# Low-rank gate products alternate over two column groups of TensorE, q0 is put between them and the second gate products, and VectorE scales five of eight columns of h

## The reference

```python
mod = (silu(cond) @ w_ada + b_ada)                       # shifts, scales, gains of each condition
h = rmsnorm(x, norm1_g) * (1.0 + sc1) + sh1
(r, k, v, lw_f, lw_b, la_f, la_b, lg, q_g, k_g, v_g, og, lgk_f, lgk_b) = split_cols(h @ w_in, IN_SPLITS)
...
for d in range(2):                                       # gated linear attention, both directions
    gk = log_sigmoid(lgk[d] @ gla_gk2[d] + gla_gk_b[d]) / 16
    o, s = gla_chunk_scan(q, k, v, gk, s0[:, d])
```

## Time and profile before

| | us |
|---|---|
| three runs before | 978.35, 982.75, 985.03 |
| median | 982.75 |
| profiled execution | 982.82 |
| its span, first to last instruction | 981.0 |
| outside the span | 1.8 |
| TensorE busy in the span | 873.4 (89%) |
| VectorE, ScalarE, GpSimdE busy | 560.7, 334.1, 146.8 |

### The profile page before, as it was taken

How to read it: one execution, slowest core, us unless ns; L and a number is a source line. 1 busy time by engine, 2 the same in 40 slices (tenths; PEclk the granted TensorE clock), 3 DMA queues, 4 the chain that set the end, 5 groups by cost and what they waited for, 6 DMA issues and landing times.

```text
span 981.0 us, 21494 instructions
## 1 busy us (share of the span) xinstructions
PE 873.4 (89%) x8900; PEld 535.9 (55%) x8900; DVE 560.7 (57%) x933; ACT 334.1 (34%) x585; POOL 146.8 (15%) x296
## 2 busy tenths in 40 slices
PE   2799999999999988778888987899994799999996
PEld 0445445655555544567777776745574354444442
DVE  1524016689967798756556664697326145554467
ACT  3222111133023758376556653312210122232223
POOL 6000101112000011334232231000001001000041
PEclk9899999999899989799999999999985799999998
DMA  9810433014224400211212211591009589999957
GB/s 330 325 64 1 134 131 102 22 69 150 87 86 172 172 1 11 40 30 31 41 32 38 49 33 49 177 363 44 33 11 342 193 276 369 369 370 368 340 125 228
DMA packets 119760, 142.46 MB, mean 145 GB/s; under 512 B 49964, under 2 KB 85224, under 8 KB 119272
## 3 DMA queue, kind: packets, MB, share of 16 engines
q1 hardware_dynamic: 110824, 116.55, 36.2%
q0 software_dynamic: 3744, 13.63, 4.5%
q10 hardware_dynamic: 5088, 10.82, 2.9%
HBM read 122.99 MB, written 18.00 MB: 144 GB/s over the span
## 4 chain that ended last, share of the span: by engine, by line
PE 78%; DVE 12%; issue 4%; ACT 3%; DMA 2%; SPq 1%; ACTq 0%; DVEq 0%; POOLq 0%
PE bank L1947 70%; PE bank L1951 8%; DVE rk_r L1406 2%; DMA region<-in_w_ada_dram 2%; ACT region L933 1%; DMA rk_r<-h_rows_dram,slot_tokens 1%; DVE region L1406 1%; DVE rk_r L1407 1%; DVE cl_b L1319 1%; DVE cl_b L1865 1%; DVE region L1936 0%; ACT w_sb L933 0%; DVE region L1350 0%; DVE region L1932 0%; ACT ada_row_buffers L933 0%
## 5 line engine op out<-in xcount | busy, mean ns | idle before, releaser
L1947 PE MATMUL bank<-region 64*64 64x64 f32 (+3 forms) x3904 | 400.6, 299 | 16.1 <-issue 7.1
L1947 PEld LDWEIGHTS bank<-region 64*64 64x64 f32 (+1 forms) x3904 | 232.5, 149 | 170.0 <-issue 159.2
L933 ACT ACTIVATE region<-bank 128x256 f32<-128x256 f32 (+3 forms) x216 | 98.1, 454 | 352.0 <-PE bank L1947 256.6
L1951 PE MATMUL bank<-ident,region 128*128 128x128 f32 (+2 forms) x403 | 67.3, 301 | 27.7 <-DMA scratch<-in_gla_gk_dram 12.6
L1947 PE MATMUL bank<-region,rk_r 128*128 128x512 f32 x176 | 80.3, 610 | 0.8 <-issue 0.8
L1951 PEld LDWEIGHTS bank<-ident,region 128*128 128x128 f32 (+2 forms) x403 | 49.6, 154 | 43.9 <-issue 34.3
L1917 DVE TENSOR_SCALAR region<-region 128x256 f32<-128x256 f32 x16 | 4.7, 294 | 100.6 <-ACT region L933 100.6
L1406 DVE SCALAR_TENSOR_TENSOR rk_r<-region,vec,rk_r 128x512 f32<-128x512 f32 x64 | 50.3, 786 | 12.3 <-ACT rk_r L933 10.2
L1947 PEld LDWEIGHTS bank<-region,rk_r 128*128 128x128 f32 x176 | 33.7, 196 | 39.7 <-issue 38.6
L908 POOL DMA_INDIRECT rk_r<-h_rows_dram,slot_tokens x16 | 15.2, 952 | 245.6 <-PE bank L1951 132.0
L1588 DVE TENSOR_TENSOR region<-bank,region 128x256 f32<-128x256 f32 x60 | 25.5, 425 | 41.5 <-PE bank L1947 40.2
(11 more groups left out here) (277 smaller groups left out, 1151.9 us busy)
## 6 DMA issues: line engine op xcount, KB each, us to landing
region<-in_moe_w_dram SPq DMA_DIRECT2D x38, 1024.0 KB, 10.3
region<-in_w_ada_dram SPq DMA_DIRECT2D x12, 2048.0 KB, 8.7
region<-in_w_in_dram SPq DMA_DIRECT2D x6, 2048.0 KB, 7.8
cl_b<-in_moe_w_dram SPq DMA_DIRECT2D x10, 1024.0 KB, 12.7
expert_rows_dram<-yg_b ACTq DMA_DIRECT2D x14, 512.0 KB, 6.8
region<-late_condition_dram SPq DMA_DIRECT2D x3, 1024.0 KB, 9.7
a_rows_dram<-region SPq DMA_DIRECT2D x20, 128.0 KB, 2.9
region<-inverse_rows_dram SPq DMA_DIRECT2D x20, 128.0 KB, 3.0
```

Of the source, the lines that this page charges most:

```text
L933: return act.activation(out, in_, func, **kw)
L1947: return pe.matmul(out, lhsT, rhs, start=start, stop=stop)
L1951: return pe.transpose(out, in_, ident[0:n, 0:n])
```

## The change

Five things change. The loop over the first gate products takes both directions of a column k before it goes to the next k, so that products for rows 0 to 15 and rows 32 to 47 of the bank alternate. The order of the columns is a list, `COLS_DONE`. ScalarE scales columns 0, 2, 4, and VectorE 1, 3, 5, 7, 6. The projection q0 stands between the first and the second gate products, on TensorE and in ScalarE's queue. The second gate products alternate over the directions too, and VectorE reads them out in that order.

```diff
-        jobs += [("lgkl",), ("lgkc",)]
-        jobs += [("gkl", d, i) for d in range(2) for i in range(GC)] + [("gkc",)]
...
+        jobs += [("lgkl",), ("lgkc",)] + unit("q0")
+        jobs += [("gkl", d, i) for i in range(GC) for d in range(2)] + [("gkc",)]
...
+        COLS = [(0, 2, 4), (1, 3, 5, 7, 6)]
+        COLS_DONE = [(1, 0), (0, 0), (1, 1), (0, 1), (1, 2), (1, 3), (0, 2), (1, 4)]
...
-            for k in range(0, KT, 2):
+            for k in COLS[0]:
...
+            qk_out("q0", 0)
             act.wait_ge(s_lgx, 1)
             act.wait_ge(s_zd, 48)
             own(A(glt, region1[:, KT * T + 2 * GC * T:KT * T + 4 * GC * T], ACT.Abs))
...
-            for n, i in (("q0", 0), ("q1", 1), ("g0", GC), ("g1", GC + 1)):
...
+            for n, i in (("q1", 1), ("g0", GC), ("g1", GC + 1)):
+                qk_out(n, i)
...
-            for k in range(1, KT, 2):
+            for k in COLS[1]:
                 if k == 1:
                     wait_result(dve, "hc", 0)
+                elif k == 6:
+                    wait_result(dve, "hl", 6)
...
-                for d in range(2):
-                    for k in range(KT):
-                        if d == 0 and key == "lgkl":
-                            pe.wait_ge(s_hT[k % 2], k // 2 + 1)
-                        ins = mm(b[32 * d:32 * d + GKL, 0:n], w_lgk[:, k, d * GKL:(d + 1) * GKL], hT[:, k, sl], start=k == 0, stop=k == KT - 1)
+                for n_, (j, m) in enumerate(COLS_DONE):
+                    k = COLS[j][m]
+                    if key == "lgkl":
+                        pe.wait_ge(s_hT[j], m + 1)
+                    for d in range(2):
+                        ins = mm(b[32 * d:32 * d + GKL, 0:n], w_lgk[:, k, d * GKL:(d + 1) * GKL], hT[:, k, sl], start=n_ == 0, stop=n_ == KT - 1)
                 finish(ins)
+            w = slab("qk")
+            project("q0", w, 0)
             wait_result(pe, "lgkl")
             wait_result(pe, "lgkc")
-            for d in range(2):
-                for i in range(GC):
+            for i in range(GC):
+                for d in range(2):
                     finish(mm(open_bank("gkl", d, i)[:, :], gk2_sb[32 * d:32 * d + GKL, i * P:(i + 1) * P], lgkT[32 * d:32 * d + GKL, P:T]))
```

More of the change, by code:

```diff
@@ L328, in slot @@
             return out
-        for n in chan:
+        for n in chan[1:]:
             jobs += unit(n)
@@ L964, in _, with qk_out @@
                 tell(A(hT[:, k, 0:P], hT[:, k, 0:P], ACT.Identity, scale=gscv[:, 0, k, 0:1], bias=modv[:, k, 0:1]), s_hT[0])
+            def qk_out(n, i):
+                sc = HD ** -0.5 if n[0] == "q" else 1.0
+                copy_out(qk_g[:, i, P:T], ("pl", n), scale=sc)
+                copy_out(qk_g[:, i, 0:P], ("pc", n), bank(("pc", n))[:, 0:P], scale=sc)
+            qk_out("q0", 0)
             act.wait_ge(s_lgx, 1)
@@ L970, in _ @@
             tell(A(glt, glt, ACT.Ln, bias=1.0), s_lgt)
-            for n, i in (("q0", 0), ("q1", 1), ("g0", GC), ("g1", GC + 1)):
-                sc = HD ** -0.5 if n[0] == "q" else 1.0
-                copy_out(qk_g[:, i, P:T], ("pl", n), scale=sc)
-                copy_out(qk_g[:, i, 0:P], ("pc", n), bank(("pc", n))[:, 0:P], scale=sc)
+            for n, i in (("q1", 1), ("g0", GC), ("g1", GC + 1)):
+                qk_out(n, i)
             def gla_exps(p):
@@ L2147, in _ @@
             w = slab("qk")
-            for i, n in enumerate(chan):
-                project(n, w, i * P)
+            for i, n in enumerate(chan[1:]):
+                project(n, w, (i + 1) * P)
             w = slab("vg")
```

## The result

The changed kernel takes 969.76 us (median of 4 runs, 967.56 to 970.52) against 980.89 us for the kernel before (median of 4, 978.35 to 985.03). The ratio is 0.9891, 95% interval 0.9859 to 0.9922: 10.7 us faster, 7.7 to 13.8. Forecast were 976.0 us and a gain of 6.8 us, with a range of 971.7 to 980.5: the direction is right, the size is not. The profiled execution took 969.55 us, with a span of 967.8 us.

A forecast was written before the change was run, and what follows sets the result against it. TensorE was taken to bound the kernel from 47.4 to 220.7 us, almost without a break. Terms -5.6 - 0.8 - 0.4 + 0 = -6.8 us, from 982.82 us, gave 976.0 us, range 971.7 to 980.5 us.

The forecast's parts named there:

- Start of the first gate products: TensorE's first gate products wait for VectorE's column 1, not ScalarE's column 0: start at 46.90 us, before 47.38 us.
- First gate products: TensorE's alternating products for two column groups run side by side and end at 57.08 us, before 62.68 us: -5.6 us.
- Rival (b): Alternating first gate products run one after another, none side by side: 984.9 us, slower than before; chance 0.06.
- Fifth column: Scaling of columns ahead of the first gate products: giving VectorE a fifth column is worth nothing.
- q0 over the standstill: Projection q0, 8.65 us, covers TensorE's 0.81 us wait for VectorE's copies between the gate products: -0.8 us.
- Second gate products: TensorE's second gate products, alternating, need four slots in place of five: -0.4 us, bounds 0 and -0.9 us.
- The second fall: Clock at half level from 67.21 to 70.62 us, behind the second gate products: assumed to stay, 0; if gone, -1.7 us.
- rival (a): The clock's second fall, behind the second gate products, does not come: 974.3 us; chance 0.25.
- Its busy stage shifts as a whole: From 220.67 us, where VectorE takes over the chain from TensorE, everything behind moves earlier by what TensorE saved.
- Rival (c): Later clock falls change in number, each costing 1.7 us: 979.4 or 972.6 us; chance 0.2, half on each side.
- The base: Starting time of the sum: the profiled execution of the kernel before, 982.82 us, 0.07 us off the median of three runs.

The follow-up runs named there:

- threefold products: The changed kernel with each of the four second gate products over latent tokens issued three times into its bank; 978.55 us, ratio 0.9972.
- q0 alone: The kernel before with one edit, projection q0 placed between the first and the second gate products; 980.23 us, ratio 1.0004.
- the pair with one product: The changed kernel with one added full-array product of 512 columns, ahead of q0's products (973.51 us) or ahead of q1's, behind the second gate products (973.58 us).
- by-direction kernel: The changed kernel with the second gate products taken by direction again, on TensorE and VectorE; 969.83 us, ratio 0.9885.
- n = 3: The changed kernel with three added full-array products of 512 columns (2.6 us) ahead of q1's; 974.15 us, ratio 0.9917.
- alternation alone: The kernel before with one edit, the first gate products taking both directions of a column before the next column; 976.28 us, ratio 0.9966.

## Why the prediction was wrong, by its own steps

**Start of the first gate products: right.** They start 0.67 us earlier (0.48 forecast); 0.2 us of that comes from the condition rows of this execution, where the clock fell at 46.55 us in place of 46.73 us.

**First gate products: right.** 10.32 us, and with the start -5.65 us, forecast -5.6. Rival (b), products one after another, is out.

**Fifth column: right**, worth nothing.

**q0 over the standstill: right but for 0.2 us.** The standstill is gone; q0 takes 8.85 us from start to start, not 8.65, which is the upper bound given for one more change between full-array and small products.

**Second gate products: wrong by 0.4 us.** "Alternating, they need four" slots: they take as many as before, 3.12 against 3.09 us, and in both orders the loads stand in the same slots. What overlaps in one order overlaps in the other. I had read the pattern from the count of slots, not from a pair of traces.

**The second fall: wrong choice.** I took 0 as likelier than -1.7 us; in the changed kernel it does not come. The reason given on the side of "falls" was right (16-row products bring it down by themselves, as the threefold products show), the one on the side of "does not" was not (a missing standstill does not keep the level up, since q0 alone between them leaves the fall). What decides, as the pair with one product shows, is where the products lie. This is rival (a), 974.3 us.

These five make up the handover: -5.65 - 0.81 + 0.2 + 0.03 - 1.71 = -7.9 us, as measured.

**"Its busy stage shifts as a whole": wrong, the failed step.** The sum put the difference behind 220 us at nothing. It is 10.7 - 7.9 = 2.8 us by the ratio, 5.3 us in the two traces. TensorE's later standstills meet the changes of clock level at other places. Rival (c) had this mechanism and left its sign open, so the sign is no merit of the forecast. 1.5 us of it is shown: behind the standstill near 255 us the kernel before is at half level for 6.8 us, the changed one for 3.4.

The rest is not settled. Of the 5.3 us in the traces, 3.8 us come late, between the starts of the same two VectorE instructions (519.02 and 600.18 us in the changed kernel, 528.68 and 613.67 us before). There the kernel before has one fall more (609.93 to 613.34 us), worth 1.7 us at most, and a pause of TensorE of 1.65 us in place of 0.55 us (at 591.82 and 580.82 us) that nothing in the profile explains. This stretch also varies without any fall in it: next to the changed kernel it is 2.8 us shorter with the threefold products and 1.5 us longer in the by-direction kernel. So half-level time alone does not give the tail: with n = 3 the changed kernel spends only 22 us at half level between 50 and 640 us, and lies on the line all the same.

**The base.** The sum was made on 982.82 us, near the median of the three runs shown. Later medians of the kernel before are 979.58 us (29 runs), 980.83 (23), 980.62 (13) and 980.57 (29), so the base was 2.2 us high, more than the 1.5 us of uncertainty in the range. The 6.2 us between the forecast and the median are, within rounding, these 2.2, 1.1 us of the front (7.9 for 6.8) and 2.8 us behind it. The time lies 1.9 us below the range, so either the base or the term behind 220 us would have been enough to carry it out.

## What to carry to other kernels

Products of 16 output rows for two column groups of the array run side by side if they alternate in the program, and one after another if all of one group come first; here this took a third off the stage (15.3 to 10.2 us). Before an engine's saving is carried to the end one to one, shift the kernel by a known amount (one full product) in both versions: here that alone moved the time by 2 to 3 us against the line, about a quarter of the change's own worth. And an order that looks serial in the source may overlap already; read the loads, not the loop.

## What the runs showed of the hardware that was not expected

The granted clock fell to half with TensorE busy throughout, when the products used 16 of 128 rows for long (70.3 to 80.6 us in the kernel with threefold products), and stayed at full through 12 us of products on all rows and 16 columns (50.1 to 62.7 us before). Once down, it stayed so for 3.4 or 6.8 us, even where full-array products followed within 1.6 us of the fall (61.0 to 67.8 us with alternation alone, 73.1 to 79.9 us with q0 alone), and for 10.2 us with the threefold products, 5.4 us of it under full-array ones. Behind one and the same standstill it was down for 0, 3.4 or 6.8 us, depending on a shift of 0.9 to 2.6 us, and the chain was 1.7 and 3 us longer for it. A kernel got 2.3 us faster (0.9977, 0.9956 to 0.9999) by 0.86 us of added work.
